# Shift, scale and h of the first normalization made in two channel halves, with the first two key tiles multiplied half by half

## The chip, the cores and the metric

The kernel runs on one core of a Trainium2 chip. The core has TensorE (PE: matmuls, and transposes written as matmuls), VectorE (DVE), ScalarE (ACT), GpSimd (POOL), and SyncE (SP), which here issues nearly all DMAs. Each engine executes its own program in order; they meet only at semaphores. The metric is the device time of one execution in microseconds (us); lower is better.

## The reference, cut to what matters

One layer of a hybrid decoder is computed for 512 prompt tokens and 8 sequences of 8 sample tokens (576 tokens), with 1024 channels. The change touches only its beginning:

```python
mod = jax.nn.silu(c) @ w_ada + b_ada                 # 9 rows of c: one prompt, eight samples
sh1, sc1, g1, sh2, sc2, g2 = jnp.split(mod, 6, axis=-1)
h = rmsnorm(x, norm_pre1) * (1 + sc1[:, None]) + sh1[:, None]
proj = h @ w_in
split_idx = [int(s) for s in np.cumsum(IN_SIZES)[:-1]]
bg, cg, ua, q, k, v, r, lr, ga, gb = jnp.split(proj, split_idx, axis=-1)
...
log_a = jax.nn.log_sigmoid((lr @ w_a2 + b_a).astype(jnp.float32)) / GLA_TAU
```

Everything behind it (gated convolution, linear attention, output projection, ConvFFN) is the same in both kernels.

## The kernel before, in words

Every large product is done in three passes on pairs of numbers: a weight tile is split into a rounded part `w_hi` and a rest `w_lo`, the activations h into `h_hi` and `h_lo`, and PE adds w_hi·h_hi, w_lo·h_hi and w_hi·h_lo. A channel tile is 128 columns of a weight matrix: 8 blocks of 128 input channels, each multiplied with two halves of 288 tokens, three passes, 48 matmuls. Weight tiles are numbered in the order of use: 0 to 3 are the columns of k, 4 to 7 those of q, then v and the rest. A tile lands in a buffer `raw`, ACT copies it rounded into `w_hi` (`high`), and POOL subtracts (`low`) to make `w_lo`; for tiles 0 and 1 DVE does that (`first_low`). SP issues the loads; `load_raw` waits on `w_lo_done` until the raw buffer is free.

The program opens with a prologue that has to make h. SP loads x (2.25 MiB, `x_tok`), then the first 2048 columns of w_ada (8 MiB, `ada_first`, shift in columns 0 to 1023 and scale in 1024 to 2047) in eight DMAs of 1 MiB, one for each block of 128 rows, with small parameter rows between them, then tile 0, `w_lr`, tile 1. PE passes from one token tile to the next in `for i in range(KT)`: eight transposes of x (L1823), which ACT copies out as `h32` (L957), and `ada_first_rows(i)` (L1808): four matmuls of 512 columns that run in four column groups of the array. `keep_warm(n)` (L1803) is n dummy transposes, there to keep PE at work. At i = 5 `parameters` (L1785 to L1790) transposes six pieces of parameter rows.

Then a chain over the engines follows: the 36 sums of each group are in rows, ACT copies them to SBUF (L959), PE transposes them back (L1833), DVE adds the bias (`mod`, L1304), makes the scale (`mul1`, L1308), scales and shifts the sample tokens of h (`h_smp`, L1328 and L1330), ACT rounds tile 0 (`high(0)`, L931), and makes `h_hi` block by block (L965, and L969 for the sample tokens of all blocks at once). The first pass of tile 0 follows block by block as h_hi comes; then come the first pass of tile 1, the second passes of both tiles (`first_pass`, L1861), the low-rank product `lr_rows` (L1846), the third pass of tile 0, `z` for head 0 (L1906), the third pass of tile 1, z for head 1, and from there whole tiles (`channel_tile`, L1874). A z for head n waits until DVE has taken that of head n-1 (`z_min`), since all four use one pair of banks; ACT reads it first (L987), DVE after it (L1343).

```python
            for p in range(2):
                for n in range(2):
                    pe.wait_ge(S("w_lo_done" if p else "w_hi_done"), n + 1)
                    first_pass(n, p)
```

## Time and profile before

| | |
|---|---|
| times of 3 runs | 1010.29, 1011.6, 1011.71 us; median 1011.6 us |
| span of the profiled execution (first to last instruction) | 1007.4 us |
| what lies around the span, against the median of the runs | 4.2 us |
| PE busy | 987.9 us, 98% of the span |
| DVE, ACT, POOL busy | 543.0, 385.9, 228.6 us |
| granted clock of TensorE | 0.999 of full speed over the span |

The profiled execution has no time of its own beside its span; the table sets the span against the median of the three timed runs. A busy PE is one whose matmuls are in flight; the share of the span tells how full the queue is, not that the array is at its peak. Idle time of an engine that nobody waits for costs nothing.

### The profile page before, as it was taken

The page shows a single profiled execution, that of the slowest core. Times are in us where ns is not written, and L with a number is a line of the kernel's source. Part 1 is how long each engine was busy: PE and PEld are TensorE (multiplying, and loading weights), DVE is VectorE, ACT ScalarE, POOL GpSimd, SP SyncE. Part 2 cuts the span into 40 slices and gives each one's busy share as a digit, 9 for nine tenths or more (in the row PEclk, how much of TensorE's full clock was granted, in tenths as well). Part 3 has the DMA queues.
Part 4 walks back from the last instruction along what each step waited for, and adds up shares of the span by engine and source line. Part 5 has one row for each costly group of instructions (what it writes and reads, how often), then busy time and mean ns, then how long its engine had stood idle before and what let it go on. Part 6 is the DMA issues. An engine that isn't in the chain of part 4 may idle for free.

```text
span 1007.4 us, 18705 instructions
## 1 busy us (share of the span) xinstructions
PE 987.9 (98%) x7743; PEld 897.7 (89%) x7743; DVE 543.0 (54%) x868; ACT 385.9 (38%) x588; POOL 228.6 (23%) x124
## 2 busy tenths in 40 slices
PE   7799999999999999999999999999999999999997
PEld 5689889999999999899998789999999999888886
DVE  2501104667555665346436688877777778750204
ACT  4532533143343334443463345333333334533212
POOL 2043433233343333233343020000000000013330
PEclk9999999999999999999999999999999999999999
DMA  9565344598366657545427042222322222323212
GB/s 354 171 93 180 116 90 96 129 115 136 106 193 165 138 128 139 91 105 160 123 91 219 1 124 86 64 85 84 85 84 85 84 85 63 126 64 100 79 59 94
DMA packets 144132, 115.59 MB, mean 115 GB/s; under 512 B 11353, under 2 KB 123761, under 8 KB 143025
## 3 DMA queue, kind: packets, MB, share of 16 engines
q1 hardware_dynamic: 143953, 114.38, 43.5%
q8 instruction: 61, 1.00, 0.4%
q14 instruction: 22, 0.18, 0.1%
q10 hardware_dynamic: 96, 0.04, 0.0%
HBM read 107.02 MB, written 7.35 MB: 114 GB/s over the span
## 4 chain that ended last, share of the span: by engine, by line
PE 93%; SPq 2%; DMA 1%; ACT 1%; DVE 1%; issue 1%; DVEq 0%
PE pair L1874 50%; PE pair L1929 16%; PE pair L2250 10%; PE pair L2203 5%; PE pair L2009 1%; PE pair L1982 1%; DMA raw<-in_w_in 1%; PE pair L1861 1%; SPq L667 1%; SPq L705 1%; PE pair L1921 1%; PE pair L2072 1%; PE pair L2061 1%; PE pair L1922 1%; PE pair L1923 1%
## 5 line engine op out<-in xcount | busy, mean ns | idle before, releaser
L1874 PE MATMUL pair<-h_hi,w_hi 128*128 128x288 f32 x1280 | 285.6, 301 | 0.1
L1874 PE MATMUL pair<-h_hi,w_lo 128*128 128x288 f32 x1280 | 279.1, 296 | 0.0
L1874 PE MATMUL pair<-h_lo,w_hi 128*128 128x288 f32 x1280 | 278.8, 295 | 0.0
L860 POOL TENSOR_TENSOR w_lo<-raw,w_hi 128x1024 fp32r<-128x1024 f32 x57 | 140.1, 2459 | 601.5 <-ACT w_hi L931 601.5
L1874 PEld LDWEIGHTS pair<-h_hi,w_hi 128*128 128x128 f32 x1280 | 207.2, 189 | 18.4 <-issue 16.3
L1874 PEld LDWEIGHTS pair<-h_lo,w_hi 128*128 128x128 f32 x1280 | 207.6, 188 | 0.0
L1874 PEld LDWEIGHTS pair<-h_hi,w_lo 128*128 128x128 f32 x1280 | 207.7, 188 | 0.0
L931 ACT ACTIVATE w_hi<-raw 128x1024 fp32r<-128x1024 f32 x70 | 73.5, 1056 | 160.5 <-PE pair L1923 75.7
L860 POOL TENSOR_TENSOR w_lo<-raw_c,w_hi 128x1024 fp32r<-128x1024 f32 x24 | 68.2, 2846 | 124.7 <-ACT w_hi L931 124.7
L1929 PE MATMUL pair<-w_hi,f_hi 128*128 128x512 f32 x176 | 68.9, 391 | 0.0
L1929 PE MATMUL pair<-w_lo,f_hi 128*128 128x512 f32 x176 | 68.7, 390 | 0.0
L1929 PE MATMUL pair<-w_hi,f_lo 128*128 128x512 f32 x176 | 68.5, 389 | 0.0
L1164 ACT ACTIVATE cv<-cv 128x592 f32<-128x592 f32 x22 | 15.4, 700 | 106.3 <-DVE cv L522 106.3
L2250 PE MATMUL pair<-t_hi,w_hi 128*128 128x288 f32 x144 | 42.5, 295 | 0.0
L2250 PE MATMUL pair<-t_lo,w_hi 128*128 128x288 f32 x144 | 42.5, 295 | 0.0
L2250 PE MATMUL pair<-t_hi,w_lo 128*128 128x288 f32 x144 | 42.4, 295 | 0.0
L1929 PEld LDWEIGHTS pair<-w_hi,f_lo 128*128 128x128 f32 x176 | 33.1, 188 | 7.0
L1929 PEld LDWEIGHTS pair<-w_hi,f_hi 128*128 128x128 f32 x176 | 33.0, 188 | 7.0
L1929 PEld LDWEIGHTS pair<-w_lo,f_hi 128*128 128x128 f32 x176 | 33.0, 188 | 6.8
L522 DVE SCALAR_TENSOR_TENSOR cv<-ext,ffp,cv 128x592 f32<-128x592 f32 x44 | 36.7, 834 | 1.6
L931 ACT ACTIVATE w_hi<-raw_c 128x1024 fp32r<-128x1024 f32 x24 | 25.2, 1055 | 26.8 <-PE pair L1874 12.0
L2250 PE MATMUL pair<-h_hi,w_hi 128*128 128x288 f32 x108 | 31.8, 294 | 0.0
(349 smaller groups left out, 1603.5 us busy)
## 6 DMA issues: line engine op xcount, KB each, us to landing
raw<-in_w_in SPq DMA_DIRECT2D x256, 64.0 KB, 3.1
raw_c<-in_w_ada SPq DMA_DIRECT2D x32, 512.0 KB, 5.8
raw_c<-in_w_in SPq DMA_DIRECT2D x192, 64.0 KB, 3.6
raw<-in_w_up SPq DMA_DIRECT2D x24, 512.0 KB, 4.7
raw<-in_w_down SPq DMA_DIRECT2D x22, 512.0 KB, 3.7
raw_up<-in_w_up SPq DMA_DIRECT2D x20, 512.0 KB, 3.8
ada_first<-in_w_ada SPq DMA_DIRECT2D x8, 1024.0 KB, 13.8
raw<-in_w_in SPq DMA_DIRECT2D x8, 512.0 KB, 4.7
```

What stands on the lines that cost most here:

```text
L522: dve.scalar_tensor_tensor(dst[:, :], src[:, tap:tap + CONV], w[tap], dst[:, :], ALU.mult, ALU.add) \
L667: sp.dma_start(dst[:, i, :], src[:, i, :]).then_inc(S(raw_name(n)), 16)
L705: sp.dma_start(ada_first[:, i, :], w_ada[P * i:P * i + P, 0:2 * D]).then_inc(S(f"ada_in{i}"), 16)
L860: pool.tensor_tensor(lo, raw_tile(n)[:, :], hi.bitcast(F32), ALU.subtract).then_inc(S("w_lo_done"), 1)
L931: act.activation(dst, raw_tile(n)[:, :], ACT.Copy).then_inc(S("w_hi_done"), 1)
L1164: act.activation(cv[:, :], cv[:, :], ACT.Gelu_apprx_tanh).then_inc(S("gelu_done"), 1)
L1861: ins = pe.matmul(bank[n][:, half, 0:HALF], w[:, i, :], x[:, i, HALF * half:HALF * half + HALF], start=i == 0 and p == 0, stop=i == KT - 1 ...
L1874: ins = pe.matmul(bank[pair][:, half, 0:HALF], w[:, i, :], x[:, i, HALF * half:HALF * half + HALF], start=i == 0 and p == 0, stop=i == KT ...
L1921: pe.matmul(dst[0:64, :], first_i[:, 0:64], wl[:, 0, :], start=False, stop=False)
L1929: ins = pe.matmul(one_bank(banks[t])[0:m, :], x, w[:, i, :], start=first and i == 0 and p == 0, stop=last and i == 1 and p == 2)
L2203: ins = pe.matmul(bank[wo_pair(x)][0:n, c, :], xx, w[:, 512 * c:512 * c + 512], start=y == 0 and p == 0, stop=y == KT - 1 and p == len(pas ...
L2250: ins = pe.matmul(dst, w[:, i, :], x[:, i, :], start=i == 0 and p == 0, stop=i == 3 and p == 2)
```

## The change

`ada_first` is laid out and loaded in two halves: half 0 holds channels 0 to 511 of shift and of scale, half 1 channels 512 to 1023 (16 DMAs of 512 KiB, with rows of 2 KiB where they were 8 KiB). `mod`, `mul1`, the sample tokens, `h_hi`, `h_lo` are made for blocks 0 to 3 first and for 4 to 7 later. Tiles 0 and 1 are loaded together (`raw01`, 256 columns) in eight DMAs of 128 KiB that ACT issues: four ahead of its copies of x, four behind its first row copy. Tiles 2 and 3 (`raw23`) have a buffer of their own and no wait. PE does all three passes of blocks 0 to 3 for both tiles, with the matmuls of ada half 1 between them, then those of blocks 4 to 7. Five of the six transposes of parameters move behind tile 5 (`late_parameters`), and the DVE copies of them behind the four `z_min`.

```diff
-            for i in range(KT):
-                sp.dma_start(ada_first[:, i, :], w_ada[P * i:P * i + P, 0:2 * D]).then_inc(S(f"ada_in{i}"), 16)
-                for dst, src in small[3 * i:3 * i + 3]:
+            def load_ada_first(half, i):
+                src = w_ada[P * i:P * i + P, 0:2 * D].rearrange("p (a h c) -> p a h c", a=2, h=2)[:, :, half, :]
+                sp.dma_start(ada_first[:, half, i, :].rearrange("p (a c) -> p a c", a=2), src) \
+                  .then_inc(S(f"ada_in{3 * half + max(0, i // 2 - 1)}"), 16)
+            for i in range(KT):
+                load_ada_first(0, i)
+                for dst, src in small[3 * i:min(3 * i + 3, 9)]:
                     sp.dma_start(dst, src).then_inc(S("rows_in"), 16)
-            load_raw(TILE_K, in_cols(IN_K))
+            for i in range(KT):
+                load_ada_first(1, i)
...
+            for i in range(KT):
+                sp.dma_start(raw23[:, i, :], w_in[P * i:P * i + P, IN_K + 2 * DK:IN_K + 4 * DK]).then_inc(S("raw_c_in2"), 16)
...
+            sp.wait_ge(S("w_lo_done"), 2)
+            for dst, src in small[9:]:
+                sp.dma_start(dst, src).then_inc(S("rows_in"), 16)
...
@@ ScalarE
+            for i in range(4):
+                act.dma_start(raw01[:, i, :], w_in[P * i:P * i + P, IN_K:IN_K + 2 * DK]).then_inc(S("raw_in1"), 16)
             for t in range(TT):
...
-            act.wait_ge(S("ada0_mm"), 1)
-            act.activation(rows_ada0[:, :], one_bank(0)[:, :], ACT.Copy).then_inc(S("rows0_done"), 1)
-            high(0)
...
+            for half in range(2):
+                first_rows(half)
+                if half == 0:
+                    for i in range(4, KT):
+                        act.dma_start(raw01[:, i, :], w_in[P * i:P * i + P, IN_K:IN_K + 2 * DK]).then_inc(S("raw_in0"), 16)
+                high_half(0, half)
+                high_half(1, half)
+                act.wait_ge(S("mul1_done"), half + 1)
+                for i in range(4 * half, 4 * half + 4):
+                    act.activation(h_hi[:, i, 0:SEQ], h32[:, i, 0:SEQ], ACT.Identity, bias=mod[:, i, 0:1],
+                                   scale=mul1[:, i, 0:1]).then_inc(S("h_hi_done"), 1)
+                    if i == 4 * half:
+                        act.wait_ge(S("h_smp"), 2 * half + 2)
+                        act.activation(h_hi[:, i:i + 4, SEQ:T], h32[:, i:i + 4, SEQ:T], ACT.Copy).then_inc(S("h_hi_done"), 1)
...
@@ TensorE
-            for i in range(KT):
-                if i < TT:
...
+            for i in range(3):
+                ada_first_rows(0, i)
+                keep_warm(6)
+            for t in range(TT):
+                x_to_channels(t)
+                ada_first_rows(0, 3 + t)
+                if t < TT - 1:
+                    keep_warm(3)
+            parameters()
+            first_back(0)
+            keep_warm(16, 7)
...
+            pe.wait_ge(S("mod_first"), 2)
+            for i in range(4):
+                pe.wait_ge(S("h_hi_done"), max(2, high_at(i)))
+                for n in range(2):
+                    pe.wait_ge(S("w_hi_half"), n + 1)
+                    first_product(0, i, n)
...
+                if i % 2:
+                    ada_first_rows(1, i - 1)
+                    ada_first_rows(1, i)
+                else:
+                    keep_warm(2, 7)
```

On PE, from the last row of ada sums to the first whole passes, the program before reads as follows (L1808 are the ada matmuls, L1833 the transposes back, L1861 the products of tiles 0 and 1, whose rounded parts are `w_hi_51` and `w_hi_52`):

```order
L1808 MATMUL pair<-ada_first,c_wide 32x512 x4
L1833 MATMUL pair<-ident,rows_ada_86 128x128 x4
L1803 MATMUL pair<-ident 128x128 x16
L1861 MATMUL pair<-h_hi,w_hi_51 128x288 x2
L1803 MATMUL pair<-ident 128x128 x3
L1861 MATMUL pair<-h_hi,w_hi_51 128x288 x2
```

In the changed program the same place has products of both tiles with ada matmuls of 256 columns between them (here L1884 ada, L1902 transposes back, L1939 products, L1879 warmers; from the first transposes back to the end of the second block):

```order
L1902 MATMUL pair<-ident,rows_ada_88 128x128 x2
L1879 MATMUL pair<-ident 128x128 x16
L1939 MATMUL pair<-h_hi,w_hi_51 128x288 x2
L1939 MATMUL pair<-h_hi,w_hi_52 128x288 x2
L1879 MATMUL pair<-ident 128x128 x2
L1939 MATMUL pair<-h_hi,w_hi_51 128x288 x2
L1939 MATMUL pair<-h_hi,w_hi_52 128x288 x2
L1884 MATMUL pair<-ada_first,c_wide 32x256 x8
```

The second half of the ada matmuls thus stands behind the first products, and the transposes back occur twice. At the head of PE's program the changed kernel has three blocks of ada ahead of the first transposes of x (L1896):

```order
L1879 MATMUL pair<-ident 128x128 x36
L1884 MATMUL pair<-ada_first,c_wide 32x256 x4
L1879 MATMUL pair<-ident 128x128 x6
L1884 MATMUL pair<-ada_first,c_wide 32x256 x4
L1879 MATMUL pair<-ident 128x128 x6
L1884 MATMUL pair<-ada_first,c_wide 32x256 x4
L1879 MATMUL pair<-ident 128x128 x6
L1896 MATMUL pair<-ident,x_tok 128x128 x8
```

Before, the transposes of x came right behind the 36 warmers; now they stand behind matmuls that wait for four ada loads (`ada_in0` is waited for at 64). On ACT the stretch behind the copies of x was this before (`rows_ada_86` is the row copy, `raw_49` tile 0):

```order
L959 ACTIVATE rows_ada_86<-pair 128x512 [waits ada0_mm]
L931 ACTIVATE w_hi_51<-raw_49 128x1024 [waits raw_in0]
L965 ACTIVATE h_hi<-h_73,mod,mul_165 128x512 [waits mul1_done,x_ch]
L965 ACTIVATE h_hi<-h_73,mod,mul_165 128x512
L969 ACTIVATE h_hi<-h_73 128x8x64 [waits h_smp]
L965 ACTIVATE h_hi<-h_73,mod,mul_165 128x512 x6
```

In the changed program it is this (L990 the row copy, L1005 the DMAs of `raw01`, L997 the halves of w_hi):

```order
L990 ACTIVATE rows_ada_88<-pair 128x256 [waits ada0_mm,x_ch]
L1005 DMA raw_64<-in_w_in 128x256 x4
L997 ACTIVATE w_hi_51<-raw_64 128x512 [waits raw_in1]
L997 ACTIVATE w_hi_52<-raw_64 128x512 [waits raw_in1]
L1010 ACTIVATE h_hi<-h_75,mod,mul_167 128x512 [waits mul1_done]
L1014 ACTIVATE h_hi<-h_75 128x4x64 [waits h_smp]
L1010 ACTIVATE h_hi<-h_75,mod,mul_167 128x512 x3
```

Four DMA issues and two rounding copies now stand between the row copy and the first block of h_hi.

## Rows read from the trace of the kernel before

**Rows 1.** Waits of PE from 61 us to the end.

```profile
PE pair L2176 <- DVE xn L618: 1.0, 1, 1.0
```

**Rows 2.** Chain that ended last, 24 to 110 us: start, length, what.

```profile
25.03 12.27 DMA raw<-in_w_in
...
38.29 1.50 ACT h_hi L965 x2
...
45.55 6.64 PE pair L1861 x48
52.20 2.08 PE pair L1846 x32
54.27 2.31 PE pair L1861 x16
56.58 0.69 PE pair L1906 x4
...
60.26 6.57 PE pair L1874 x48
```

**Rows 3.** Timeline of PE, 7 to 36 us: start, length, instructions, idle before.

```profile
7.12 6.39 PE L1803 MATMUL pair<-ident 128*128 128x128 f32 x36
14.08 1.06 PE L1823 MATMUL pair<-ident,x_tok 128*128 128x128 f32 x8 [0.57 <-DVE x_tok L1289]
15.08 1.06 PE L1808 MATMUL pair<-ada_first,c_wide 128*32 128x512 f32 x8
16.07 0.87 PE L1803 MATMUL pair<-ident 128*128 128x128 f32 x6
16.79 1.04 PE L1823 MATMUL pair<-ident,x_tok 128*128 128x128 f32 x8
...
24.90 0.71 PE L1823 MATMUL pair<-ident,x_tok 64*128 64x64 f32 x8
...
29.30 0.46 PE L1790 MATMUL pair<-ident,rows_ff 128*128 128x128 f32 x3
...
32.97 1.06 PE L1808 MATMUL pair<-ada_first,c_wide 128*32 128x512 f32 x8 [0.65 <-DMA ada_first<-in_w_ada]
34.76 0.66 PE L1833 MATMUL pair<-ident,rows_ada 128*128 128x128 f32 x4 [0.72 <-ACT rows_ada L959]
```

**Rows 4.** Timeline of ACT, 0 to 60 us; ACTq is its issuing of DMAs.

```profile
1.43 0.60 ACTq L934 DMA_DIRECT2D rows_c<-in_c_sample  x1
...
34.11 0.60 ACT L959 ACTIVATE rows_ada<-pair 128x512 f32<-128x512 f32 x1 [7.87 <-PE pair L1808]
37.33 1.06 ACT L931 ACTIVATE w_hi<-raw 128x1024 fp32r<-128x1024 f32 x1 [2.62 <-DMA raw<-in_w_in]
...
40.22 4.34 ACT L965 ACTIVATE h_hi<-h,mod,mul 128x512 fp32r<-128x512 f32 x6
...
57.31 0.74 ACT L987 ACTIVATE suf<-pair,prm 128x576 f32<-128x576 f32 x1
```

**Rows 5.** Timeline of DVE, 29 to 60 us.

```profile
35.45 0.31 DVE L1304 TENSOR_TENSOR mod<-pair,prm 128x144 f32<-128x144 f32 x1 [4.58 <-PE pair L1833]
...
36.06 0.69 DVE L1328 TENSOR_TENSOR h<-h,mul 128x512 f32<-128x512 f32 x1
...
58.16 0.82 DVE L1343 TENSOR_SCALAR pre<-pair,prm 128x576 f32<-128x576 f32 x1 [8.73 <-ACT suf L987]
```

**Rows 6.** Tile ada_first: its DMAs (ns min/median/max) and their landing (us).

```profile
L705 SPq DMA_DIRECT2D ada_first<-in_w_ada x8: 351/436/1977, 3.5 to 15.6; - x8
...
DMA to landing us min/median/max: 9.0/13.8/17.4
```

**Rows 7.** Windows: stretch, busy times; the last three are clock, DMA share, GB/s.

```profile
14.00:30.00 16.00, 15.37 (x128) 9.23 (x129) 2.77 (x5) 4.69 (x5) 0.00 (x0) 1.00 1.02 406
...
877.00:877.50 0.50, 0.50 (x4) 0.41 (x3) 0.00 (x0) 0.00 (x0) 0.00 (x0) 1.00 0.98 381
72.50:73.00 0.50, 0.50 (x6) 0.50 (x5) 0.00 (x0) 0.00 (x0) 0.08 (x1) 1.00 1.03 72
```

**Rows 8.** Timeline of SP, 0 to 130 us: issuing of tile 1's loads.

```profile
28.44 9.89 SPq L667 DMA_DIRECT2D raw<-in_w_in  x8
```

More of the change, by code:

```diff
@@ L312, in high_at, with pair_tile @@
     def high_at(i):
-        return i + 1 if i < 2 else i + 2
+        return (1, 3, 4, 5, 6, 8, 9, 10)[i]
+    def pair_tile(n, blocks=slice(0, KT)):
+        return (raw01, raw23)[n // 2][:, blocks, P * (n % 2):P * (n % 2) + P]
     def c1_pair(j, i):
@@ L865, in _ @@
             for n in (2, 3):
-                low(n, w_hi[n][:, :], w_lo[n][:, :], n + 1)
+                low_of_pair(n)
             with pool.Fori(1, TILE_C1 // 4) as g:
@@ L970, in _, with first_rows, high_half @@
-            high(1)
-            act.wait_ge(S("h_hi_done"), KT + 1)
+            def first_rows(half):
+                act.wait_ge(S("ada0_mm"), half + 1)
+                act.activation(rows_ada0[:, 256 * half:256 * half + 256], one_bank(4 * half)[:, 0:256], ACT.Copy) \
+                   .then_inc(S("rows0_done"), 1)
+            def high_half(n, half):
+                act.wait_ge(S("raw_in0" if half else "raw_in1"), 16 * HEADS)
+                blocks = slice(4 * half, 4 * half + 4)
+                act.activation(kc(w_hi[n])[:, blocks, :], pair_tile(n, blocks), ACT.Copy) \
+                   .then_inc(S("w_hi_done" if half else "w_hi_half"), 1)
@@ L1310, in _, with first_low, first_mod @@
-            dve.wait_ge(S("mul1_done"), 1)
+            def first_low(n, half):
+                dve.wait_ge(S("w_hi_done" if half else "w_hi_half"), n + 1)
+                blocks = slice(4 * half, 4 * half + 4)
+                dve.tensor_tensor(kc(w_lo[n])[:, blocks, :], pair_tile(n, blocks), kc(w_hi[n])[:, blocks, :].bitcast(F32),
+                                  ALU.subtract).then_inc(S("w_lo_done" if half else "w_lo_half"), 1)
+            def first_mod(half):
+                dve.wait_ge(S("back0"), half + 1)
+                src = one_bank(5 if half else 2)[:, 0:256].rearrange("p (b g s) -> p g b s", b=2, g=4)
+                for part in (1, 0):
+                    at_ = 8 * part + 4 * half
+                    dve.tensor_tensor(mod[:, at_:at_ + 4, :].rearrange("p (g b) s -> p g b s", g=2),
+                                      src[:, 2 * part:2 * part + 2, :, 0:9],
+                                      spread(prm[:, at_:at_ + 4].rearrange("p (g b) -> p g b", g=2), 9), ALU.add) \
+                       .then_inc(S("mod_done" if half > part else "mod_first"), 1)
@@ L1878, in channel_tile, with z_rows @@
                     ins.then_inc(S("ring_free"), 1)
+            def z_rows(n):
+                pe.wait_ge(S("lr_done"), 1)
+                pe.wait_ge(S("a2_in"), 64)
+                if n > 0:
+                    pe.wait_ge(S("z_min"), n)
+                for half in range(2):
+                    side = slice(64 * half, 64 * half + 64)
+                    ins = pe.matmul(bank[3][:, half, 0:HALF], w_a2[side, DK * n:DK * n + DK], lr[side, :],
+                                    start=True, stop=True)
+                ins.then_inc(S("z_mm"), 1)
@@ new lines, in _ @@
+            for n in range(2):
+                pe.wait_ge(S("w_lo_half"), n + 1)
+                for i in range(4):
+                    first_product(1, i, n)
+                if n == 1:
+                    ada_first_rows(1, 4)
+                    ada_first_rows(1, 5)
+            for i in range(4):
+                pe.wait_ge(S("h_lo_done"), i + 1)
+                for n in range(2):
+                    first_product(2, i, n)
+            ada_first_rows(1, 6)
+            ada_first_rows(1, 7)
@@ new lines, in _ @@
+            first_back(1)
+            keep_warm(16, 7)
+            pe.wait_ge(S("mod_done"), 1)
+            for i in range(4, KT):
+                pe.wait_ge(S("h_hi_done"), max(7, high_at(i)))
+                for n in range(2):
+                    pe.wait_ge(S("w_hi_done"), n + 1)
+                    first_product(0, i, n)
+                keep_warm(2, 7)
+            for n in range(2):
+                pe.wait_ge(S("w_lo_done"), n + 1)
+                for i in range(4, KT):
+                    first_product(1, i, n)
@@ L1892, in _ @@
                 if n < 2:
-                    first_pass(n, 2)
+                    for i in range(4, KT):
+                        pe.wait_ge(S("h_lo_done"), i + 1)
+                        ins = first_product(2, i, n)
+                    ins.then_inc(S("ring_free"), 1)
                 else:
@@ L1898, in _ @@
                     channel_tile(kc(w_hi[n % 4]), kc(w_lo[n % 4]), n % 3, (h_hi, h_lo))
+                if n == 5:
+                    late_parameters()
                 if n < 4:
-                    pe.wait_ge(S("lr_done"), 1)
-                    pe.wait_ge(S("a2_in"), 64)
-                    if n > 0:
-                        pe.wait_ge(S("z_min"), n)
-                    for half in range(2):
-                        side = slice(64 * half, 64 * half + 64)
-                        ins = pe.matmul(bank[3][:, half, 0:HALF], w_a2[side, DK * n:DK * n + DK], lr[side, :],
-                                        start=True, stop=True)
-                    ins.then_inc(S("z_mm"), 1)
+                    z_rows(n)
             def token_tiles(n, g, banks, x_hi, x_lo, first, last, done, tiles=range(TT), smp=None):
```

185 lines of the change are left out of this document (97 added, 88 removed).

## The prediction

> **What bounds the kernel now.** I read the waits of PE first. From 61 us to the end they name a single wait of 1.0 us [rows 1]: behind the prologue PE is never short of work, so a change in the prologue is worth exactly the time by which it moves the start of tile 2, the first whole tile, at 60.26 us [rows 2], plus whatever it adds to PE's program later. Nothing behind that start hangs on an absolute time: the raw buffers come free as PE advances, and the prefetch moves with it.
>
> Then the chain of work that ended last, in its first 60 us [rows 2]. Backwards from tile 2 it is PE alone down to 45.55 (48 products in 6.64 us, so 0.139 us a matmul of 288 columns; the low-rank product 2.08; third passes 2.31 each; z 0.69 each). Ahead of that ACT makes h_hi from 38.29 on, and ahead of ACT the chain waits for tile 0, whose last load lands at 37.30. The timeline of ACT says the same: the rounding of tile 0 at 37.33 stood idle 2.62 us for a DMA [rows 4]. So before the change two things end almost together: the 8 MiB of w_ada, whose last matmuls start at 32.97, released by a DMA [rows 3], and tile 0 behind them in the same queue. In the windows the DMA engines are full (share 1.02, 406 GB/s) from 14 to 30 us [rows 7]. The granted clock is 1.00 there and in every window shown, so both kernels are costed at that clock.
>
> **What PE has to gain.** While it waits for w_ada and for the chain behind it (from 34.03, the end of the last ada matmuls, to 45.55) PE does no product beside those of tile 0's first pass. The change puts half of the products of tiles 0 and 1 ahead of the second half of the ada matmuls. The matmuls themselves are not saved, only moved into waiting time. What it costs is a second pass through the chain over the engines, and everything that is moved ahead of the first pass. I follow the chain of the changed kernel from its start to tile 2.
>
> **Step 1, the start of ada half 0.** Its first matmuls wait for four loads of half 0, and the transposes of x, which began at 14.08 [rows 3], stand behind three blocks of it. The first MiB of w_ada landed at 3.45 + 9.0 = 12.45 [rows 6]. The changed kernel needs 2 MiB there. Rows of 2 KiB are new in this place; in the down projection such rows come at 381 GB/s with a share of 0.98 [rows 7], against 406 for the 8 KiB ones, so the second MiB takes 2.75 us: 15.2. ACT's first four DMAs of raw01 (512 KiB) are issued at about 13 and share the same full engines; between nothing and their whole 1.4 us I take 0.8. Start: **16.0**. The warmers end at 13.5 [rows 3], so PE now stands still for 2.5 us here.
>
> The Trainium skill (DMA: Bandwidth & Descriptors, "Issuing engines are not separate DMA queues") says that DMAs issued from several engines run on the same 16 DMA engines and interleave, and that only sequencer time is saved. By that rule all of raw01's first half would push w_ada back in proportion to what interleaves, and the sum's 0.8 would be between 0.7 and 1.4; the window's share of 1.02 agrees that there is no room left.
>
> **Step 2, to the end of half 0's ada sums.** Eight transposes of x take 1.00 (14.08 to 15.08), four ada matmuls of 512 columns 0.99 (15.08 to 16.07), six warmers 0.72 (16.07 to 16.79) [rows 3]. For 256 columns I halve all but a fixed 0.13: 0.56, between the bounds 0.5 and, if nothing shrank, 0.99. Three times (0.56 + 0.72) = 3.84, to 19.84. Four token tiles of 1.00 + 0.56 + 0.36 = 1.92 make 7.7, to 27.5; the last tile, of 64 tokens, takes 0.64 (its 0.71 less the 0.07 by which such rows overlap [rows 3]) + 0.56, to **28.7**. The loads are ahead of this: half 0 complete needs 2 MiB more than at 16.0, 5.5 us, that is 21.5 to 22.5, and its last two blocks are wanted at 26.5. So the order on PE bounds this stretch, not the DMA.
>
> **Step 3, from the sums to the first product.** Row copy: 0.60 for 512 columns [rows 4], 1.06 for 1024 [rows 4], so 0.38 for 256, plus 0.1 hand-over: 29.2. Then ACT issues four DMAs. The trace has its own two at 0.60 to 0.62 each [rows 4] and those of SP at a median of 0.44 with some 0.05 between them [rows 6]; I take 0.5 for tables of 128 rows: 2.0, to 31.2 (bounds 1.9 and 2.5). Two half roundings, 0.5 each and 0.1 at the end: 32.3. In the meantime PE transposes back and DVE makes mod, scale and samples, done by 31.1, so ACT is the late one, and the four issues stand on the path in full: without them the first h_hi would start near 30.3. First block of h_hi 0.71 (4.34 for six [rows 4]), sample copy 0.3: the first product starts at **33.3**, which I call A.
>
> **Step 4, PE behind A.** 48 products of 0.139 = 6.7; the eight ada blocks of half 1, in pairs, 1.0 a pair = 4.0; four warmers 0.5; some 0.2 for changes of form: 11.4. The feeders are faster: h_hi comes each 0.71 while a block with its ada pair takes 1.6; DVE has its eight operations on h and two on w_lo (0.5 to 0.75 each) done by A + 5.7, wanted at A + 8.2. Half 1's last loads land at 22.0 + 4 MiB at 381 GB/s (11.0) + the other 512 KiB of raw01 (1.4 to 3) = 34.4 to 36, wanted at A + 10.4 = 43.7: hidden by 7 us. This step ends at **44.7**; before, the last ada matmuls ended at 34.03.
>
> **Step 5, the second pass through the chain.** Row copy 0.5, transposes back 0.45 (half of 0.66 [rows 3] and a fixed part), three DVE operations of 36 columns at 0.2 (0.31 for 144 [rows 5]): 46.3. Samples twice 0.42 (0.69 for twice the columns [rows 5]) and ACT's copy 0.35: PE resumes at 47.5. Three more blocks of h_hi, 2.1, and the last block's products and warmers 0.8: 50.5. From 44.7 to 50.5 PE does only 16 products, 2.2 us: this is the second hole, 3.6 us, which the change adds.
>
> **Step 6, to tile 2.** Second passes 2.2, low-rank product 2.1, third pass of tile 0 1.1, z 0.7: 56.6. Now z of head 1 comes late. Before, 2.31 us of third pass lay between the two z; now it is 1.1. From the end of the first z ACT's read and DVE's take 1.7 (57.27 to 58.98, from the last rows of ACT and DVE [rows 4, 5]), so head 1 starts at 58.3 and not at 57.7. Its 0.7: tile 2 starts at **59.0** against 60.26. That is 1.2 less.
>
> **Step 7, what comes later.** Five parameter transposes on a PE that is now full: three take 0.46 [rows 3], five 0.6. Their DVE copies lie between tiles 5 and 8, where DVE waits for ACT. SP's six small loads, now behind the second w_lo at about 48.5, delay tiles 4 and 5 by 2.1, to about 57 and 60; PE wants tile 4 at 73. Tiles 2 and 3 no longer wait for raw buffers, and are rounded by ACT at 52 and 56: hidden. If that cover were gone each us would count in full.
>
> **Sum:** -1.2 + 0.6 = -0.6 us. The profiled span of 1007.4 becomes 1006.8; with the 4.2 between span and median, 1011.0 us. What a measurement of this kernel can tell from no change is about 0.2%, 2.0 us.
>
> **Rivals.**
> *The front comes sooner, faster.* If ACT's packets don't hold up w_ada and the queue already holds part of the second MiB when x is through (406 GB/s are moving, and 12.45 is when the first MiB was complete, not when the next began), the first four loads could be there at 14.1 instead of 16.0. All steps behind follow one for one, and at 0.45 an issue step 3 gives 0.2: -2.7, 1008.9; with another 0.5 to 1 out of hand-overs that I rounded up, 1008. For it: PE and ACT bound steps 2 to 5, not bandwidth, so nothing swallows it. Against: the share of 1.02.
> *ACT's issues are held as SP's are, slower.* With full queues SP needed 9.89 us for eight loads, 1.24 each [rows 8], and up to 1.98 for one of w_ada [rows 6]. At 29.2 SP is still pushing w_lr and tiles 2 and 3 into full queues. If ACT, in a queue of its own, pays 1.24 too, step 3 grows by 4 x 0.74 = 3.0: +2.4, 1014.0; at 1.98 it is 1017. It decides from 1.15 an issue on. Against it: ACT's queue is empty at that time. The Trainium skill (DMA: Bandwidth & Descriptors, "Queues, rings and completion order") speaks for it: SP and ACT have a ring each on every DMA engine, but not a descriptor generator of their own. No row here shows both issuing against full queues.
> *The short rows are slow, slower.* Loads of 512-byte rows moved 72 GB/s at a share of 1.03 [rows 7]. If the 1 KiB rows of raw01 came at twice that, 144 GB/s, the 1 MiB would take 7.3 us of full engines, of which up to 3 fall before the start of step 2 instead of 0.8: +2.2 - 0.6 = +1.6, and with the second part after A still hidden. With ada's 2 KiB rows slowed as well (300 GB/s, +0.7) it is 1014.
> *The change doesn't shorten the path:* then the two holes just balance, 1011.6.
>
> **How the numbers follow.** My forecast (with steps off by up to 1.5 in sum) 0.40; balance 0.04; front sooner 0.30; issues held 0.17; short rows slow 0.09. The forecast and the balance lie within 0.2%, 1009.6 to 1013.6; a small part of each outer case falls inside too: faster 0.30, same 0.45, slower 0.25. The range leaves one in ten on either side: 1007.0 to 1015.3.
>
> **What the profile would show.** Step 1: idle time of PE in front of the first ada matmul, released by a DMA, and its start near 16.0. Step 3: four issue rows on ACT of 0.5 each (held: over 1.15), and the first product at 33.3. Step 4: ada half 1 released by no DMA, end at 44.7. Step 5: a hole of PE that ends near 47.5. Step 6: a wait of z for DVE of 0.6, and tile 2 at 59.0. The forecast is wrong if tile 2 starts outside 57 to 61, or if PE has waits behind it that it had not before.

## The result

The changed kernel takes 1016.28 us (median of 7 runs, 1015.44 to 1019.94), the kernel before 1010.98 (7 runs, 1009.29 to 1014.26): ratio 1.0059, 95% interval 1.0046 to 1.0073. It is slower by 5.3 us, and outside the range of the prediction.

In every run of the changed kernel, and in all 140 runs of the kernel before that were timed beside the experiments, the time is the span plus 1.7 to 1.8 us. The profiled run of the kernel before, with its span of 1007.4, would thus be one of about 1009.2 us, at the fast end of its runs (the fastest of its seven is 1009.29); the changed kernel's was 1016.57 (span 1014.8), near its median. Of the 7.4 us between the two spans 5.1 lie ahead of tile 2 and 2.3 behind its start.

Timeline of PE after, answering [rows 3] (start, length, instructions, idle before and who ended it; L1879 warmers, L1884 ada, L1902 transposes back, L1939 products of tiles 0 and 1):

```profile
6.83 5.77 PE L1879 MATMUL pair<-ident 128*128 128x128 f32 x36
16.33 0.64 PE L1884 MATMUL pair<-ada_first,c_wide 128*32 128x256 f32 x8 [3.74 <-DMA ada_first<-in_w_ada]
16.90 1.43 PE L1879 MATMUL pair<-ident 128*128 128x128 f32 x6
18.25 1.08 PE L1884 MATMUL pair<-ada_first,c_wide 128*32 128x256 f32 x8
...
30.33 0.64 PE L1884 MATMUL pair<-ada_first,c_wide 128*32 128x256 f32 x8
30.90 0.33 PE L1856 MATMUL pair<-ident,rows 124*128 124x124 f32 x1
31.54 0.44 PE L1902 MATMUL pair<-ident,rows_ada 128*128 128x128 f32 x2 [0.31 <-ACT rows_ada L990]
31.81 1.91 PE L1879 MATMUL pair<-ident 128*128 128x128 f32 x16
37.22 1.01 PE L1939 MATMUL pair<-h_hi,w_hi 128*128 128x288 f32 x4 [3.50 <-ACT h_hi L1014]
38.04 0.63 PE L1879 MATMUL pair<-ident 128*128 128x128 f32 x2
38.32 1.31 PE L1939 MATMUL pair<-h_hi,w_hi 128*128 128x288 f32 x4
39.56 1.74 PE L1884 MATMUL pair<-ada_first,c_wide 128*32 128x256 f32 x16
41.22 0.79 PE L1939 MATMUL pair<-h_hi,w_hi 128*128 128x288 f32 x4
...
50.88 0.44 PE L1902 MATMUL pair<-ident,rows_ada 128*128 128x128 f32 x2 [0.51 <-ACT rows_ada L990]
...
53.42 0.76 PE L1939 MATMUL pair<-h_hi,w_hi 128*128 128x288 f32 x4 [0.35 <-issue]
```

The reader is to compare equal rows: six warmers take 1.43 us at 16.90 and 0.87 before [rows 3], and the same 16 ada matmuls take 1.74 at 39.56 and 1.07 later. Both slow places stand behind a rest of PE, of 3.74 and 3.50 us. The windows name the reason (the last three columns are clock, DMA share, GB/s, as in [rows 7]):

```profile
16.30:18.00 1.70, 1.67 (x14) 1.21 (x14) 0.40 (x1) 0.00 (x0) 0.00 (x0) 0.72 1.06 372
18.00:20.00 2.00, 2.00 (x14) 0.94 (x13) 0.00 (x0) 0.00 (x0) 0.00 (x0) 0.50 0.67 206
...
35.00:37.20 2.20, 0.00 (x0) 0.01 (x1) 0.35 (x1) 2.20 (x5) 0.00 (x0) 1.00 0.94 222
37.20:38.00 0.80, 0.78 (x4) 0.80 (x5) 0.80 (x3) 0.80 (x2) 0.00 (x0) 0.72 0.86 297
38.00:40.00 2.00, 2.00 (x14) 1.48 (x17) 2.00 (x4) 1.24 (x2) 0.00 (x0) 0.50 1.02 334
40.00:41.00 1.00, 1.00 (x16) 0.38 (x8) 1.00 (x3) 0.00 (x0) 0.00 (x0) 0.52 0.54 125
41.00:44.00 3.00, 3.00 (x36) 2.03 (x29) 1.64 (x3) 0.00 (x0) 0.00 (x0) 1.00 0.04 12
```

Twice the granted clock goes to 0.50, 1.2 instead of 2.4 GHz, and comes back some 4 us later. The Trainium skill (TensorE: Matmul & The Clock Gate, "What's actually happening") says "the default state is throttled, and activity releases the throttle"; the trace agrees, with 0.50 behind each of the two rests and 1.00 again behind steady work.

Timeline of ACT, answering [rows 4] (L990 row copy, L1005 the four DMAs, L997 half roundings):

```profile
31.10 0.38 ACT L990 ACTIVATE rows_ada<-pair 128x256 f32<-128x256 f32 x1
31.11 3.80 ACTq L1005 DMA_DIRECT2D raw<-in_w_in  x4
34.96 1.15 ACT L997 ACTIVATE w_hi<-raw 128x512 fp32r<-128x512 f32 x2 [3.48 <-issue]
36.02 0.80 ACT L1010 ACTIVATE h_hi<-h,mod,mul 128x512 fp32r<-128x512 f32 x1
```

The four issues take 3.80 us where 2.0 were reckoned; in the chain of waits three of their pieces read 0.46, 0.65 and 2.28, so one was held, that is, it took far longer than the others. At that time SP issued the loads of tiles 2 and 3 (timeline of SP, as [rows 8]):

```profile
25.81 11.29 SPq L730 DMA_DIRECT2D raw<-in_w_in  x8
```

Landing of `ada_first`, answering [rows 6]: 16 DMAs of half the size, the last issued at 23.3.

```profile
L716 SPq DMA_DIRECT2D ada_first<-in_w_ada x16: 390/884/2349, 3.4 to 23.3; - x16
...
  DMA ada_first<-in_w_ada: 3.7, 1
...
DMA to landing us min/median/max: 7.5/11.9/14.1
```

PE waited for it once, 3.7 us, in front of the first block; half 1 was hidden. Then the end of the prologue, in the chain that ended last [rows 2], and the DVE piece that answers to `pre` of [rows 5]:

```profile
63.68 0.83 DVE pre L1409
64.51 0.14 issue
64.64 0.76 PE pair L1963 x4
65.40 4.71 PE pair L1949 x34
```

Tile 2 starts at 65.40 instead of 60.26. And the waits of PE from 61 us on, answering [rows 1]:

```profile
PE pair L1949 <- issue: 1.8, 1, 1.8
PE pair L2295 <- DVE xn L627: 1.0, 1, 1.0
PE pair L2101 <- issue: 0.6, 1, 0.6
PE pair L1963 <- DVE pre L1409: 0.6, 1, 0.6
```

The row for xn was there before. That of L1963 is z's wait, as predicted. The two with "issue" are new: 2.4 us, in 220 to 240 and at 273.5, in which PE waits and the profile shows nobody whom it waits for.

### The profile page after: what moved, and what is told of

The parts are those of the page before. It is cut to its first block, busy times and chain, and to the rows that moved or that the text cites. A ratio compares the mean times of both kernels' runs of the same rounds, so it can differ in the third digit from the quotient of the medians.

```text
span 1014.8 us, 18829 instructions
## 1 busy us (share of the span) xinstructions
PE 990.1 (98%) x7799; PEld 899.0 (89%) x7799; DVE 544.3 (54%) x876; ACT 386.2 (38%) x592; POOL 230.0 (23%) x124
## 4 chain that ended last, share of the span: by engine, by line
PE 95%; DVE 1%; ACT 1%; issue 1%; DMA 1%; SPq 1%; ACTq 0%; DVEq 0%
PE pair L1949 50%; PE pair L2047 16%; PE pair L2369 10%; PE pair L2322 5%; PE pair L2128 1%; PE pair L2101 1%; PE pair L1939 1%; PE pair L1884 1%; PE pair L1879 1%; DMA ada_first<-in_w_ada 1%; PE pair L2039 1%; PE pair L2180 1%; PE pair L2191 1%; PE pair L2040 1%; PE pair L2041 1%
## 5 line engine op out<-in xcount | busy, mean ns | idle before, releaser
L1949 PE MATMUL pair<-h_hi,w_hi 128*128 128x288 f32 x1280 | 285.3, 300 | 0.1
L1949 PE MATMUL pair<-h_hi,w_lo 128*128 128x288 f32 x1280 | 278.7, 295 | 1.8 <-issue 1.8
L879 POOL TENSOR_TENSOR w_lo<-raw,w_hi 128x1024 fp32r<-128x1024 f32 x55 | 135.2, 2460 | 554.9 <-ACT w_hi L958 554.9
L958 ACT ACTIVATE w_hi<-raw 128x1024 fp32r<-128x1024 f32 x66 | 69.3, 1056 | 154.1 <-PE pair L2041 75.7
L2369 PE MATMUL pair<-h_hi,w_lo 128*128 128x288 f32 x108 | 31.8, 294 | 0.0
```

The costliest lines, as they stand in the source:

```text
L879: pool.tensor_tensor(lo, raw_tile(n)[:, :], hi.bitcast(F32), ALU.subtract).then_inc(S("w_lo_done"), 1)
L958: act.activation(dst, raw_tile(n)[:, :], ACT.Copy).then_inc(S("w_hi_done"), 1)
L1949: ins = pe.matmul(bank[pair][:, half, 0:HALF], w[:, i, :], x[:, i, HALF * half:HALF * half + HALF], start=i == 0 and p == 0, stop=i == KT ...
L2369: ins = pe.matmul(dst, w[:, i, :], x[:, i, :], start=i == 0 and p == 0, stop=i == 3 and p == 2)
```

## The experiments

My theory after this result: (a) PE's rests ahead of the first ada block and ahead of the first product let its clock fall, about 1.9 and 1.7 us; (b) ACT's issues are held because SP pushes into full queues, 1.8 us; (c) the waits behind tile 2, 2.4 us, are something else. Rivals: the slow matmuls come from their operands or the DMA traffic, not from the rest; the first four loads land late whatever PE does; the late parameters or the new loads cause (c). All edits are to the changed kernel unless said otherwise. The kernel before was timed beside each group (medians 1011.0 to 1011.8).

**Filling the rests.** e1: the first `keep_warm(36)` becomes 62. e2: the `keep_warm(16, 7)` behind `first_back(0)` becomes 44. e3: both.

> The changed kernel with 62 instead of 36 warmers at PE's start, so that PE does not rest from 12.6 us until the first four ada loads are in. Theory (clock): after 3.7 us of rest the granted clock fell to 0.5 from 16.9 to 20.8 us and stretched some 3.9 us of work to twice its length; with the rest filled the clock stays at 1.00, the three ada steps take 1.3 us each instead of up to 2.4, tile 2 starts at 63.5 us instead of 65.4, and the time falls by 1.9 us. Rival (the stretch is slow for another reason, the full DMA engines or the first use of the loaded rows): the steps stay as long as they were, tile 2 stays at 65.4, no gain.

> The changed kernel with 44 instead of 16 warmers behind the first transposes back, so that PE does not rest from 33.7 to 37.2 us. Theory (clock): the fall to 0.5 from 37.5 to 41.0 us goes, the first products and the first ada pair of half 1 take 3.5 us less half of that, tile 2 starts at 63.7 us instead of 65.4 and the time falls by 1.7 us. Rival (the first pass is paced by ScalarE's h_hi at 0.71 us a block, so a slow PE costs nothing there): the clock stays up, but tile 2 moves by less than 0.5 us.

> Both rests filled with warmers. Theory (clock): the two gains add, 3.6 us, tile 2 starts at 61.8 us, and the kernel is 1 to 2 us slower than the one before instead of 5. Rival (the second loss hides behind other work): 1.9 us only, tile 2 at 63.5.

e1: 1010.04 us (1009.62 to 1012.24, 11 runs), ratio 0.9987 (0.9974 to 1.0). The first ada block came at 16.17, as before the edit (16.33), so the load and not PE had set it; but now

```profile
18.00:20.00 2.00, 2.00 (x23) 1.31 (x20) 0.00 (x0) 0.00 (x0) 0.00 (x0) 1.00 0.71 230
```

the clock is 1.00 in this window where it was 0.50, with the same operands and loads. The stretch from the first ada block to the last one of half 0 shrank from 14.00 to 12.44 us. The four issues took 1.79, the second rest shrank to 1.48, no second fall followed, and tile 2 started at 60.15. One number of warmers took 6.8 us off the profiled span, 5.2 of them ahead of tile 2; the other 1.6 lie behind, where the waits for "issue" are gone too (more on them below). e2: 1012.96 (12 runs), 1.0008 (0.9996 to 1.0021): the first fall stays (0.50 from 18 to 20 us), the second is gone, tile 2 at 63.26. e3: 1012.11 (11 runs), 1.0007 (0.9999 to 1.0016): the 44 warmers in the second place ended later than h_hi was ready (issues only 1.78 here), the first product at 35.61, tile 2 at 62.28. Theory (a) holds. The rival of operands and DMA traffic falls with e1's window. The rival of the late loads is true of the wait: the first block starts at 16.2 to 16.4 in e1, e2 and the changed kernel, whatever PE does ahead of it. It does not explain the slow work behind it. With both rests filled e3 is still no faster than e1, because the added warmers themselves ended late: the first 62 ended at 17.0 here and at 16.0 in e1.

**The issues.** e4 issues all eight DMAs of `raw01` ahead of the copies of x. e6 keeps them in place and makes SP wait.

```diff
 e4 @@ ScalarE
-            for i in range(4):
+            for i in range(KT):
                 act.dma_start(raw01[:, i, :], ...)
...
-                if half == 0:
-                    for i in range(4, KT):
-                        act.dma_start(raw01[:, i, :], ...)
 e6 @@ SyncE, ahead of w_lr and raw23
+            sp.wait_ge(S("h_hi_done"), 1)
```

> The changed kernel with all eight loads of raw01 issued by ScalarE ahead of its copies of x, and none at its first row copy. Theory (the four issues stood on the path for 3.8 us, one of them held 2.3 us by the full queues): the first product starts at about 34.0 us plus what the earlier packets delay the ada loads (0 to 1.4 us), PE's rest in front of it is about 1 us, so the second fall of the clock goes too; tile 2 starts at 60.5 to 62 us and the time falls by 3.5 to 5 us. Rival (ScalarE would have waited for DVE anyway): first product near 37, no gain. Rival (the loads now hold up ada half 0 by their whole length): the first ada matmul starts 1.4 us later and a third of the gain is lost.

> The changed kernel with SyncE waiting for the first block of h_hi before it issues w_lr and tiles 2 and 3, so that it pushes nothing into the queues while ScalarE issues the second half of raw01. Theory (ScalarE's issue is held because SyncE is pushing into full queues): the four issues take 1.8 us instead of 3.8, PE's rest is 1.5 us, the second fall of the clock goes, tile 2 starts near 62 us instead of 65.4. Rival (the hold has to do with the loads in flight, not with who issues): one issue still takes 1.6 us or more, tile 2 at 63.5 to 65.4.

e4: 1012.33 (11 runs), 1.0017 (1.0004 to 1.003). The first ada block still came at 16.23, so 512 KiB more in front cost it nothing; row copy to first product is 3.0 us instead of 6.1, tile 2 at 60.59 although the first fall stays. e6: 1013.1 (12 runs), 1.0022 (1.0006 to 1.0037):

```profile
31.03 1.80 ACTq L1006 DMA_DIRECT2D raw<-in_w_in  x4
```

With SP silent the same four issues in the same place take 1.80, 0.45 each, and none is held; the second rest is 1.50 and the second fall is gone. This alone does not show that SP is the cause, since the four were just as free with SP pushing in e1 (1.79), e3 and e5 (1.78 each). The traces say more. In the changed kernel the held issue of ACT ran beside a held issue of SP, and the two ended within 0.2 us of each other:

```profile
32.27 2.44 SPq L730 DMA_DIRECT2D raw<-in_w_in  x1
32.64 2.28 ACTq L1005
```

In e2, where the four took 2.95, it was 1.75 of SP from 32.34 on and 1.61 of ACT from 32.51 on. In e5 all four of ACT fell inside one single issue of SP, 7.62 us long from 25.02 on, and were free. So theory (b) holds in its first part, that the issues on ACT's path cost the time (e4); that a hold comes with SP's own is seen in two traces and was not brought about at will.

**Both repairs, and the order of the first work.** e7 is e1 and e4 together. e5 leaves the number of PE's instructions nearly alone and puts the first transposes of x ahead of the ada blocks, so that no rest arises. e9 is e5 with e4. e10 is e9 with 20 fewer warmers (2 for 6 between the last blocks, 3 for 5 between the first transposes).

```diff
 e5 @@ TensorE
-            for i in range(3):
-                ada_first_rows(0, i)
-                keep_warm(6)
-            for t in range(TT):
-                x_to_channels(t)
-                ada_first_rows(0, 3 + t)
...
+            for t in range(2):
+                x_to_channels(t)
+                keep_warm(5)
+            for t in range(2, TT):
+                ada_first_rows(0, t - 2)
+                x_to_channels(t)
+            for i in range(3, KT):
+                ada_first_rows(0, i)
+                if i < KT - 1:
+                    keep_warm(6)
```

> The changed kernel with the first two token tiles of x transposed ahead of the first ada matmuls and the rest of ada half 0 behind (x0, x1, then ada 0 and x2, ada 1 and x3, ada 2 and x4, then ada 3 to 7 with six warmers between). Theory (PE's own order, not the loads, set the end of half 0's sums): PE rests 1.3 us instead of 3.7, the clock stays at 1.00, the sums end near 27.5 us instead of 30.9, and tile 2 starts 3 to 5 us earlier, at 60 to 62 us. Rival (the last loads of half 0 come only by then): the sums end at 29 or later, with PE waiting for a DMA.

> The changed kernel with 62 warmers at the start and all eight loads of raw01 issued ahead of the copies of x. Theory (clock and issues are separate losses): the front alone had tile 2 at 60.5 us with the first fall of the clock still in it; without that fall it is 58.7 us, 1.5 us ahead of the kernel before, and the time 1009.5 to 1010 us, 0.1% below it. Rival (the issues were harmless once PE is busy): the same as with the warmers alone, 60.1.

> The changed kernel with the transposes of the first token tiles ahead of the ada blocks and with all eight DMAs of raw01 issued ahead of the copies of x. If the rest of PE and the issues on the path are the two separate faults of the change, their repairs add: no fall of the clock, first product near 30.8 (32.3 with the order alone), tile 2 at 57.4, 1.5 us earlier than with the order alone, time 1008.4. If the earlier issues only push back the loads of ada, a wait for them on PE appears ahead of the first product or behind it and the time stays at 1009.9.

> The same, with 16 fewer warmers between the last ada blocks and 4 fewer between the first transposes. With the clock kept, the stretch to the end of the sums is PE's own work and shrinks by 20 times 0.12 = 2.4 us: tile 2 at 55.0, time 1006.0. If the loads of ada bound it instead, waits for them take the place of the warmers and tile 2 stays above 56.5. If fewer warmers let the clock fall, it shows 0.5 ahead of tile 2 and the time is 1008 or more.

e5: 1009.9 (11 runs), 0.9987 (0.9977 to 0.9997), tile 2 at 59.01. e7: 1008.77 (7 runs), 0.9971 (0.996 to 0.9982), tile 2 at 59.88 and not 58.7: row copy to first product is 3.0 us instead of e1's 4.1, but the 62 warmers ended at 17.0 and held up the first ada block by 0.85. e9: 1008.8 (7 runs), 0.9974 (0.9963 to 0.9985); first product at 31.26, tile 2 at 57.94, 1.1 earlier than in e5, so here the repairs add. Yet e9's stretch behind tile 2 is 949.4 us, e7's 947.5, with 1.7 us of waits for "issue" in e9 and none in e7. e10: 1011.31 (12 runs, 1006.72 to 1017.85), 1.0012 (0.9992 to 1.0032):

```profile
27.28 0.85 PE L1881 MATMUL pair<-ada_first,c_wide 128*32 128x256 f32 x8 [3.30 <-DMA ada_first<-in_w_ada]
```

With fewer warmers PE reaches the last loads of half 0 3.3 us too early, rests, and loses its clock (0.50 from 27.6 to 34.4 us). In e9 the same block ran at 26.11, and a weight load of PE waited 0.2 us for the same DMAs. So here lies the limit of the front: the bytes of half 0, which are there at 26.1 to 27.3 when all of `raw01` is issued ahead of them.

**Does the kernel before lose its clock too?** In [rows 7] it does not, but most of its other runs list a clock of 0.996 to 0.998. Edits to the kernel before, in the `keep_warm(16)` behind its transposes back: e8 takes it out, e11 makes it 42, e13 29. e12 makes the first `keep_warm(36)` 62.

> The kernel before, without its 16 warmers behind the transposes back, so that PE rests about 5 us there instead of 3.3. Theory (a rest of over 3.3 to 3.5 us lets the clock fall, in any kernel): the granted clock is 0.5 for 3 to 4 us from about 41 us on, the eight first blocks of tile 0 take 1.2 us each instead of 0.6 and fall behind ScalarE's 0.71, tile 2 starts 1 to 2.5 us later than 60.2. Rival (the falls belong to the changed kernel's mix of ada matmuls and products): the clock stays at 1.00 and tile 2 at 60.2.

> The kernel before with 42 instead of 16 warmers behind the transposes back, which fills its rest of 3.3 us ahead of the first product. If its ordinary runs lose the clock behind that rest (its profiled run did not), the median falls by 1.5 to 2 us, to about 1009.5, and the clock of its runs rises to 0.999. If its ordinary runs keep the clock as the profiled one did, the time stays at 1011.3 or rises by the overrun of the warmers, up to 0.5.

> The kernel before with its first 36 warmers made 62: as many instructions of PE are added as in the kernel before with 42 warmers behind the transposes back (1014.7), but at another place, and the rest of 3.3 us ahead of the first product stays. If what made that kernel slow is where PE's later instructions stand in its stream, this one shows the same waits of PE for no releaser near 235 and 288 us, and its median is 1013 or more. If it was what the warmers do in the rest (they move the first product or tile 0), this one has no such waits and its median is 1011 to 1012.3, the upper end if the longer start (up to 1.6 us later transposes of x) reaches tile 2.

> The kernel before with 29 warmers behind the transposes back, half of what was added there. If the later waits hang on the position of the instructions, they may be gone or elsewhere, and with a rest of some 1.7 us the clock keeps up: median 1009.5 to 1010.5, clock above 0.998. If the added warmers themselves cost, the median lies between 1011.1 and 1014.7, near 1013.

e8: 1010.68 (11 runs), 0.9992 (0.9983 to 1.0001): its rest of 5.50 us (to 40.52) brings a clock of 0.50 from 38.6 to 45.4 us and tile 2 at 62.27, 2.0 later than in the profile before, and still its median is that of the kernel before. The 3.3 to 3.5 us written down for e8 do not hold as a limit: e6 lost its clock behind a rest of 3.23. e12 kept the rest (4.28 us in its profile) and shows the fall as well, in the first products, 0.82 us where e11 has 0.50:

```profile
41.43 0.82 PE L1861 MATMUL pair<-h_hi,w_hi 128*128 128x288 f32 x2 [4.28 <-ACT h_hi L969]
...
PE pair L1982 <- issue: 2.6, 2, 1.8
```

e11 filled the rest, and the clock of its runs rose to 0.997 to 0.999; but it took 1014.74 (7 runs), 1.0032 (1.0019 to 1.0045), where I had expected 1009.5. Both theories missed. Of its 3.6 us over the kernel before some 0.8 lie outside the span: in e11 and e12, and in no other kernel, the time is up to 3.5 us more than the span. Its profile has waits for "issue" of 1.4 us in 220 to 240 and at 289. e12, as many instructions more but at another place, was as slow, 1014.58 (12 runs), 1.0032 (1.0014 to 1.0051), with 2.6 us of them, in 215 to 235 and 275 to 295. e13: 1012.44 (11 runs), 1.0007 (0.9996 to 1.0019), with 2.5 us. The kernel before and e8 have none. What e11, e12 and e13 share is that PE's later instructions stand 13 or 26 places further on. Tile 2 starts later in them as well (61.07 to 62.43), but that does not sort the kernels: e8 starts it at 62.27 and has no such wait, e9 at 57.94 and has 1.7 us. The 1012.44 of e13 is near the 1013 written down for the rival, that added warmers themselves cost; e14 to e16 below speak against it, since there more instructions take waits away.

**The shift alone.** Of the changed kernels those with 16 fewer to 4 more PE transposes ahead (e10; the changed kernel itself, e4, e6; e5, e9) have 0.7 to 2.4 us of these waits, those with 26 to 54 more (e1, e2, e3, e7) none; the text below says 0 to 20 fewer, which is a miscount. With the very same stream of PE (the changed kernel, e4, e6) the waits are 2.4, 1.4 and 0.7 us, so the position tells whether they come and not how long they are. e14 and e15 (to e9) shift without filling a rest, and e16 (to e9) keeps the warmers.

```diff
 e14, e15 @@ TensorE behind first_back(1)
-            keep_warm(16, 7)
+            for _ in range(42):
+                pe.transpose(one_bank(7)[0:32, 0:32], ident[0:32, 0:32], ident[0:32, 0:32])
 e16 @@ behind each of the two keep_warm(16, 7)
+            for _ in range(14):
+                pe.transpose(one_bank(7)[0:32, 0:32], ident[0:32, 0:32], ident[0:32, 0:32])
```

> The changed kernel with the 16 warmers behind its second transposes back made 42 small ones of 32x32, which should take about as long (1.9 us, unless one takes over 0.05 us) and move all later instructions of PE 26 places on. If the waits of PE for no releaser behind tile 2 (2.4 us) hang on where its instructions stand in their stream: in the changed kernels those with 0 to 20 fewer PE transposes ahead had 0.7 to 2.4 us of them, those with 26 to 54 more had none, so here they are gone and the time falls by 1.5 to 2.4 us, to about 1014.2. If they come with the change itself (its late parameters, its loads), they stay and so does the time, 1016.3.

> The same padding in the kernel with the transposes of x first and all DMAs of raw01 issued ahead (1008.8). By position: its 1.7 us of waits without a releaser go, the stretch behind the start of tile 2 shrinks from 949.4 to 947.7, time 1007.1. By the other theory it stays at 1008.8.

> The transposes of x first, all DMAs of raw01 issued ahead, and 14 small transposes of 32x32 added behind each of the two groups of 16 warmers (28 in all, 0.033 us each by the padded kernels, 0.46 a group, of which the waits of 0.38 and 0.36 behind the groups take up most). The large warmers stay, so the clock stays at 1.00 to tile 2: start at 58.1. By the position of PE's instructions the waits for no releaser stay away and the stretch behind is 947 to 947.6: span 1005.4, time 1007.1. If the shift of 28 brings other waits than the shift of 26 did, they show as such, and the time is 1008.5 or more.

All waits of PE of e14 behind 60 us:

```profile
PE pair L2296 <- DVE xn L627: 1.0, 1, 1.0
PE pair L1963 <- DVE pre L1409: 0.6, 1, 0.6
```

The waits for "issue" are gone, and from the start of tile 2 to the end it is 947.6 us instead of 949.4. e14 takes 1012.38 (12 runs, 1009.67 to 1016.46), 1.0017 (0.9998 to 1.0036). That is more than the shift alone gives: in its profiled run the first rest was 2.98 and the clock stayed at 1.00, with no issue held (1.96 for four), and the small transposes brought a fall of their own:

```profile
46.24 1.40 PE L1995 MATMUL pair<-ident 32*32 32x32 f32 x42
...
50.00:52.00 2.00, 2.00 (x11) 1.97 (x10) 0.69 (x1) 1.97 (x4) 0.00 (x0) 0.50 0.33 93
```

PE was busy there with 42 transposes of 32x32 and lost its clock all the same (their size was not tested alone: they also end sooner than 16 large ones, 1.40 us against 1.91, and a wait of 0.77 follows). e15: 1008.08 (12 runs), 0.9971 (0.9956 to 0.9986): no wait for "issue", 946.7 behind tile 2 instead of 949.4, but the same new fall, tile 2 at 59.68 and not 57.94. e16, with its large warmers kept: 1007.66 (5 runs, 1006.77 to 1008.35), 0.9962 (0.9948 to 0.9975), clock 1.00 in all its windows from 14 to 52 us, tile 2 at 58.37, 947.5 behind it. Its median is the lowest of all, 0.4 below e15's, and by its ratio 3.8 us below the kernel before. How much of this the change's own idea is worth stays open. Against the profiled run of the kernel before, which kept its clock (about 1009.2 by its span), the profiled run of e16 is 1.5 us faster, and no run has the kernel before with its rest filled and without waits for "issue".

**Where such a wait ends.** The traces hold one thing more. The page of the profile lists a DMA queue q8 of the kind "instruction", 62 packets of 16 KiB in the changed kernel. The longest wait for "issue" lies beside one of them, which starts at 271.3 and takes 0.93 us:

```profile
273.51 0.42 PE L1949 MATMUL pair<-h_hi,w_lo 128*128 128x288 f32 x2 [1.85 <-issue]
q8 instruction: 1, 0.02, 2.4%
```

PE goes on 2.19 us after that start. It is the same each time: all 15 waits for "issue" behind tile 2 (two in the changed kernel, one each in e4, e5, e6 and e10, two each in e9, e11 and e12, three in e13) end 2.17 to 2.44 us after the start of a packet of q8, while these packets come 3 to 19 us apart there. The wait for xn, which has a releaser, ends 1.7 to 23 us after one. In the kernels without waits the packets are there as well.

## Why the prediction was wrong

Tile 2 was forecast for 59.0 and came at 65.4: 6.4 us, to be found in the steps. Behind it 1.6 more were lost. Together that is the 8.0 us between the span forecast (1006.8) and the one measured (1014.8); 2.7 of it the frame below gave back (4.2 were added to the span, and the median stands 1.5 above the profiled one), which leaves the 5.3 of the miss.

- **"both kernels are costed at that clock"** is the sentence that failed. I read 1.00 in windows in which PE hardly rested [rows 7], made a rest of 2.5 us myself in step 1 and one of about 3 in step 3, and priced both as mere waiting. Behind the first rest (3.74 in the trace, since the warmers ended at 12.6 and not 13.5) the sums ended at 30.9, not 28.7: 0.3 of it came from step 1, 1.6 is the clock (14.00 us against e1's 12.44), and 0.3 step 2 itself had too little. Behind the second, step 4 took 13.2 us instead of 11.4, of which 1.5 is the clock (11.7 in e1 and e9; from the first product to tile 2 it is 28.2 us, and 26.7 in e1, e2, e3 and e9). Filling the rests gave both back.
- **Step 3** priced an issue at 0.5 and had the held one as a rival that "decides from 1.15 an issue on". Free issues are 0.45 (e6), better than reckoned; in the profiled run one was held, sum 3.80, 0.95 each on average. So the rival's mechanism occurred, short of the size at which it was to decide. Its cost is larger than its own 1.8 us: in e1, e6 and e14, where no issue was held, the second rest was 1.48 to 1.66 and the second fall stayed away. The two faults feed each other.
- **Step 2** also had the loads of half 0 complete at 21.5 to 22.5, 4 us ahead of PE. Nothing waited for them in the changed kernel, but e9 and e10, with 512 KiB more in front, show them at 26.1 and 27.3: there was far less to spare than said.
- **Right were** step 1 (16.3 against 16.0), the 11.4 of step 4 where the clock stands (e9: 31.26 to 42.94, 11.7), the hidden half 1 of ada, step 5 (6.05 against 5.8) and z's wait of 0.6. The rival of short rows is out: neither `raw01` nor ada half 1 was waited for.
- **Small terms:** e1 has the clock and the issues as forecast, its first product at 33.48 (33.3 was said), and yet tile 2 at 60.15 and not 59.0. Steps 4 to 6 were rounded down by 1.0 in sum. Without either fault the change would only have balanced, 60.15 against 60.26.
- **Step 7** counted 0.6 for the late parameters and nothing else, because [rows 1] shows one wait. The stretch behind the start of tile 2 is 946.7 to 947.9 us in the seven changed kernels without waits for "issue", and 947.1 and 946.0 in the kernel before and e8, so the runs can neither confirm the 0.6 nor refute it. In the changed kernel it is 949.4; the 1.5 to 2.7 more are the waits that a shift of PE's instructions makes or removes (e11 to e16). That the profile before had none of them was a property of where its instructions stood.
- **The frame:** the 4.2 us between span and median were no constant but 1.75, and 2.4 of a fast profiled run. Much of this goes with the clock: the kernel before rests 3.3 us from 37.16 on, most of its runs list a lower clock than its profiled one, and e11, which fills the rest, raised it. Of its 140 runs beside the experiments the 40 that list 0.998 or more have a median of 1010.6 us, the 54 that list 0.996 or less one of 1011.9. Against such runs the change loses less than against that profile.

What stays open: why PE waits at these places. The waits are shown to come and go with the position of its instructions, and each ends at nearly the same distance from a packet of q8, so a late fetch of instructions is the likely cause. What is missing is a run that moves such a packet by itself, and the reason why it starts when it does. The DMA engines are not full there: the stretch at 272 to 274 us has them at a share of 0.80 and 271 GB/s. The Trainium skill (CRC Debugging, "Comparing the Two Runs") names queue 14 for the instruction-refill DMAs; the page of the profile gives the kind "instruction" to q14 and to q8, and the packets beside the waits are on q8. Open is also why e11's ordinary runs are up to 5 us above its profiled one (1011.58, the fastest of its seven, median 1014.74) at a clock of 0.997 to 0.999.

## What to carry to other kernels

A planned rest of PE is not free waiting: where an edit makes one as long as those that here were followed by half the clock, price the work behind it at half clock too, and fill it, with reordered real work rather than dummies (e5 against e1), and with full-size ones where it must be dummies (e15's small ones lost the clock, e16's large ones kept it). Keep DMA issues off the path of an engine that computes while another engine pushes loads; issue them where that engine idles. And judge a prologue edit by two numbers, the start of the first steady tile and the stretch behind it: if the second changes with no releaser named, a pad of cheap instructions tells whether it is only the position.

## What the runs showed of the hardware

- Rests of 3.74 and 3.50 us (the changed kernel), 3.80 (e2), 3.36 (e4), 3.23 (e6) and 4.28 (e12) went with a clock of 0.50 for about 3.4 us, rests of 3.30 (e10) and 5.50 (e8) with one of about 6.8 us; rests of 2.98 (e14) and 1.48 (e1) with none. The profiled run of the kernel before kept 1.00 behind a rest of 3.29, longer than the 3.23 that lost it in e6, so the length of the rest alone does not decide; most other runs of that kernel list a lower mean clock.
- 42 transposes of 32x32 in 1.40 us, followed by a wait of 0.77, did not hold the clock (e14: 0.50 at 50 to 52 us); 16 of 128x128 in 1.91 us at the same place did.
- A DMA issued by ACT costs 0.45 us when its way is free (four in 1.80), and one cost 2.28 beside an issue of SP that took 2.44.
- 13 to 28 transposes more ahead brought 1.4 to 2.6 us of PE waits some 200 us later (e11 to e13), or took 1.7 to 2.4 us of them away (e14 to e16).
- All 15 waits of PE for "issue" behind tile 2, of 0.27 to 1.85 us, end 2.17 to 2.44 us after the start of a 16 KiB packet on q8, the queue of the kind "instruction".
